# Block 1's attention, context squares and last key and query rotations re-divided among the engines of a two-block kernel

## The chip, the cores and the metric

One core of one Trainium2 chip runs the kernel. The metric is the device time of one execution in microseconds (us), the median of several runs. The engines are TensorE (PE in the rows, PEld for its weight loads), VectorE (DVE), ScalarE (ACT), GpSimd (POOL) and the queue of SyncE (SPq), which issues most DMAs.

## The reference

256 tokens of width 2048 go through two transformer blocks in fp32. The first block is the one whose attention the change touches:

```python
h = rms_norm(x, pre_mix_g[l])
z = h @ w_in[l]                       # q, k, v (8 heads of 128) and u (1024 wide)
a = chunked_attention(q, k, v, rel_bias[l])   # chunks of 64, scores * 128**-0.5 + bias
p = multiscale_pool(u, pool_w[l], pool_scale[l])  # trailing means over 2, 4, 8, 16 tokens minus the token, then a 256x256 map per group
m = jnp.concatenate([a, p], axis=-1) @ w_o[l]
x = x + rms_norm(m, post_mix_g[l])
h = rms_norm(x, pre_ffn_g[l])
up = causal_dwconv(h @ w_up[l], conv_w[l], conv_b[l])
y = (gelu(up[..., :D_FF]) * up[..., D_FF:]) @ w_down[l]
x = x + rms_norm(y, post_ffn_g[l])
```

The bias is added to the scaled scores and depends on query minus key position alone, clipped at 128 either way. The second block takes x and a context of 256 tokens: both are normalized and modulated (six vectors from `silu(c) @ w_ada`), keys and values of both come from w_in2, keys and queries are normalized per head and rotated (rope), 16 heads attend with a softmax (branch A) and 8 with a difference of two softmaxes (branch B), two gated branch products are added and go through w_out, and a gated feed-forward follows.

## The kernel before

Everything is kept with features on the partitions: an activation is 16 tiles of 128x256. Each weight matrix is read in units of 128x1024 (`raw`, 512 KB) into a ring of four. ScalarE rounds a unit to fp32r (`whi`, line 560), VectorE takes the rest (`wlo`, line 1027), and TensorE multiplies: high by high, high by low and low by high, 24 products a unit (lines 1622 to 1624, or 1608 to 1611 where a stage puts both halves in one PSUM bank). A `Stage` is one weight matrix or a part of it; its body is one turn of a loop over output groups. Each engine walks the same list of stages, and for unit j+4 it works while TensorE multiplies unit j. Work that is not a weight product is put between the units by hand. A DMA of a unit waits for the low half of the unit that had its slot. VectorE also makes the modulation vectors from `cond_rows`, one 128x512 fused product and sum at a time (line 1170, `condition`), against four vectors of silu; the last of them, `cond_silu_tail`, lies in the PSUM bank `CT`.

**Block 1's attention** stands between the stages w_in and w_o. TensorE, when the last group of w_in is evacuated, turns the values (line 1676, 16 transposes, copied out by ScalarE in line 737). VectorE scales the queries (line 1298, `q_scaled`). Then 16 steps follow, one per head h and block of 128 queries b; step i has 128 keys for b=0 and 256 for b=1. The score is two products into one PSUM bank, queries by keys (line 1686) and a product of a flipped identity with a Hankel matrix of the bias (line 1688). VectorE reduces to the negated maximum (line 1313), ScalarE takes exp with its sum (line 746), VectorE the reciprocal (1306) and the multiply (1308), TensorE transposes the result (1700) and issues the score of step i+2, ScalarE copies (754), TensorE multiplies by the values (1711), and a finished head is split into its high (758) and low half (1318). In VectorE's queue the multiply of step i-1 stands ahead of the reduction of step i:

```python
if 1 <= i <= N:
    n = i - 1
    dve.wait_ge(exped, n + 1)
    dve.reciprocal(...)
    dve.tensor_scalar(R[:, 48 + n % 2, 0:w], ...).then_inc(probs, 1)
if i < N:
    dve.wait_ge(scored, i + 1)
    dve.tensor_reduce(SM[:, i % 2:i % 2 + 1], PS[:, i % 2, 0, 0:w], AX.X, ALU.max, negate=True)
```

GpSimd makes the pooled means of the four groups meanwhile (lines 493 to 503). After the last step TensorE does 8 pool products (line 1720), one at a time with ScalarE's high half (761) and VectorE's low half (1271) of each; TensorE waits for all 16 operand tiles, and w_o starts.

**Context squares.** In stage up1c ScalarE squares the context (line 800). GpSimd adds the 16 tiles of squares up to one in 8 operations (line 519), and TensorE sums that over partitions in the last body of stage up1b.

**Rotations.** In stage q (48 units, steps 0 to 47) and in stage gates (steps from 48 on) keys and queries come in 12 chunks. A rotation of a chunk needs its halves swapped by DMAs and is three operations, chunk by cosine, swapped by sine, and their sum. VectorE rotates chunks 6, 0, 7, 1, 8, 9 (`rotate`, lines 1419 to 1423), GpSimd chunks 2, 3, 4, 5, 10, 11 (`rotate_late`, lines 541 to 546). Chunks 10 and 11, of 128x1024, are branch B's queries. Branch A's scores begin at step 55 (line 1831), its softmax on VectorE in lines 1470 to 1480, its transposes on TensorE in line 1816. Branch B's scores begin at step 87.

**First branch.** Stage branch_a is a loop of four bodies of two groups; VectorE evacuates each group with line 1079. TensorE's `body` waits at a body's first group for one evacuation more than elsewhere, since in the first body the group before belongs to the gates, and for the operand tiles:

```python
pe.wait_ge(evac_done, group(st, b, gb) + (2 if st is st_ba and fresh and gb == 0 else 1))
```

## Time and profile before

| | |
|---|---|
| median of 3 runs | 2875.73 us (2875.54 to 2875.75) |
| profiled execution, its own time | 2876.91 us |
| its span | 2875.1 us, granted clock 0.994 |
| PE busy | 2811.4 us (98%), 19046 products |
| DVE / ACT busy | 1997.1 us (69%) / 1274.9 us (44%) |
| POOL busy | 86.0 us (3%) |
| DMA | 612.77 MB, 213 GB/s |
| `wlo` on DVE, one | 1233 ns, x864 |
| `whi` on ACT, one | 1060 ns, x864 |

A view of the trace gives a start in us from the span's beginning, a length, an engine, the line of the kernel, the operation and its tiles; in square brackets stands how long the engine was idle before it, and which engine's event ended the wait. A row with x8 merges eight instructions.

### The profile page before, as it was taken

How to read it: one execution, taken by the hardware profiler on the slowest of the kernel's cores; microseconds unless marked ns; L12 is line 12 of the kernel's file. 1: busy time of each engine (PE TensorE's matmuls, PEld its weight loads, DVE VectorE, ACT ScalarE, POOL GpSimd, SP SyncE). 2: the span in 40 equal slices, each digit the busy share in tenths (PEclk: the TensorE clock that was granted, in tenths of full speed). 3: DMA queues.
4: the chain of work that ended last, by engine and by line, in shares of the span. 5: the costliest groups of instructions: out<-in, count | busy, mean ns of one | idle time of the engine just before them, and what ended most of it. 6: DMA issues, size and time to landing. Idle time of an engine off the chain costs nothing.

```text
span 2875.1 us, 52879 instructions
## 1 busy us (share of the span) xinstructions
PE 2811.4 (98%) x19046; PEld 2575.8 (90%) x19046; DVE 1997.1 (69%) x3060; ACT 1274.9 (44%) x1587; POOL 86.0 (3%) x74
## 2 busy tenths in 40 slices
PE   8998899999999999999999999999989999999999
PEld 8998899998899988888889898899988888888888
DVE  6776789867799987666678667866665555555554
ACT  5344455544454444211344455654444444344443
POOL 0011000100000000000003100000000000000000
PEclk9999999999999999999999999999999999999999
DMA  8874678667888885577777655666656666666665
GB/s 306 273 246 126 214 264 275 192 181 247 258 265 273 275 269 174 178 239 241 263 228 246 209 168 159 211 186 181 183 154 185 188 186 187 188 184 187 186 188 163
DMA packets 211744, 612.77 MB, mean 213 GB/s; under 512 B 23472, under 2 KB 31792, under 8 KB 210992
## 3 DMA queue, kind: packets, MB, share of 16 engines
q1 hardware_dynamic: 199296, 591.49, 65.9%
q10 hardware_dynamic: 11008, 14.60, 1.6%
q0 software_dynamic: 1328, 5.24, 0.5%
q8 instruction: 64, 1.05, 0.1%
q14 instruction: 48, 0.39, 0.0%
HBM read 600.75 MB, written 5.77 MB: 211 GB/s over the span
## 4 chain that ended last, share of the span: by engine, by line
PE 88%; DVE 6%; issue 3%; DMA 2%; ACT 1%; DVEq 0%; SPq 0%; ACTq 0%
PE acc L1624 24%; PE acc L1620 24%; PE acc L1622 12%; PE acc L1623 12%; DMA cond_rows<-w_ada 2%; PE acc L1608 2%; PE acc L1610 2%; PE acc L1611 2%; PE sums L1823 1%; PE acc L1618 1%; DVE cond_rows L1170 1%; PE acc L1831 1%; DVE wlo L1027 1%; PE turned L1816 1%; PE acc L1617 1%
## 5 line engine op out<-in xcount | busy, mean ns | idle before, releaser
L1027 DVE TENSOR_TENSOR wlo<-raw,whi 128x1024 fp32r<-128x1024 f32 x864 | 1064.2, 1233 | 713.9 <-ACT whi L560 711.5
L560 ACT ACTIVATE whi<-raw 128x1024 fp32r<-128x1024 f32 x864 | 914.6, 1060 | 1363.0 <-PE acc L1624 1132.4
L1624 PE MATMUL acc<-operand,wlo 128*128 128x256 f32 (+1 forms) x4816 | 1396.3, 290 | 0.0
L1622 PE MATMUL acc<-operand,whi 128*128 128x256 f32 (+1 forms) x3136 | 925.7, 295 | 29.2 <-DVE wlo L1027 14.0
L1624 PEld LDWEIGHTS acc<-operand,wlo 128*128 128x128 f32 x4816 | 921.8, 191 | 14.6
L1623 PE MATMUL acc<-operand,whi 128*128 128x256 f32 (+1 forms) x3136 | 923.9, 295 | 0.0
L1622 PEld LDWEIGHTS acc<-operand,whi 128*128 128x128 f32 x3136 | 603.4, 192 | 43.7 <-issue 25.4
L1623 PEld LDWEIGHTS acc<-operand,whi 128*128 128x128 f32 x3136 | 603.4, 192 | 12.7
L1620 PE MATMUL acc<-operand,whi 128*128 128x512 f32 x1680 | 599.9, 400 | 6.1 <-DVE operand L1385 5.7
L1620 PE MATMUL acc<-ffn_act,whi 128*128 128x512 f32 x1344 | 472.0, 395 | 0.0
L1620 PEld LDWEIGHTS acc<-operand,whi 128*128 128x128 f32 x1680 | 316.7, 189 | 81.7 <-issue 6.8
L1624 PE MATMUL acc<-ffn_act,wlo 128*128 128x256 f32 x1344 | 376.9, 280 | 0.0
L1620 PEld LDWEIGHTS acc<-ffn_act,whi 128*128 128x128 f32 x1344 | 252.0, 187 | 57.9
L1624 PEld LDWEIGHTS acc<-ffn_act,wlo 128*128 128x128 f32 x1344 | 254.0, 189 | 1.4
L1170 DVE CUSTOM_DVE_ANT_0 cond_rows<-cond_rows,cond_silu,cond_sums 128x512 f32<-128x512 f32 x252 | 191.5, 760 | 8.4 <-DMA cond_rows<-w_ada 6.4
L1608 PE MATMUL acc<-operand,whi 128*128 128x256 f32 x512 | 160.6, 314 | 0.0
L1611 PE MATMUL acc<-operand,wlo 128*128 128x256 f32 x512 | 145.0, 283 | 0.0
L1610 PE MATMUL acc<-operand,whi 128*128 128x256 f32 x512 | 144.9, 283 | 0.0
L1608 PEld LDWEIGHTS acc<-operand,whi 128*128 128x128 f32 x512 | 98.2, 192 | 20.3 <-issue 19.5
L1610 PEld LDWEIGHTS acc<-operand,whi 128*128 128x128 f32 x512 | 98.2, 192 | 8.2 <-issue 8.2
L1611 PEld LDWEIGHTS acc<-operand,wlo 128*128 128x128 f32 x512 | 98.1, 192 | 0.0
L1170 DVE CUSTOM_DVE_ANT_0 cond_rows<-cond_rows,cond_silu_tail,cond_sums 128x512 f32<-128x512 f32 x126 | 93.6, 743 | 6.3 <-DMA cond_rows<-w_ada 4.6
(220 smaller groups left out, 2005.2 us busy)
## 6 DMA issues: line engine op xcount, KB each, us to landing
cond_rows<-w_ada SPq DMA_DIRECT2D x512, 256.0 KB, 4.3
raw<-w_in SPq DMA_DIRECT2D x224, 512.0 KB, 3.6
raw<-w_up SPq DMA_DIRECT2D x176, 512.0 KB, 4.5
raw<-w_down SPq DMA_DIRECT2D x88, 512.0 KB, 3.7
raw<-w_fg SPq DMA_DIRECT2D x88, 512.0 KB, 3.8
raw<-w_fu SPq DMA_DIRECT2D x88, 512.0 KB, 3.5
raw<-w_fd SPq DMA_DIRECT2D x88, 512.0 KB, 3.5
raw<-w_o SPq DMA_DIRECT2D x32, 512.0 KB, 3.8
```

Source lines behind the costliest of these rows:

```text
L560: act.activation(whi[j % RING][:], raw[j % RING][:], ACT.Copy).then_inc(hi_done, 1)
L1027: dve.tensor_tensor(wlo[j % RING][:], raw[j % RING][:], whi[j % RING][:].bitcast(F32), ALU.subtract).then_inc(lo_done, 1)
L1170: dve.tensor_tensor_reduce(out=rows, in0=rows, in1=(staged_parts if st is st_up1c else silu_parts)[kr], scale=1.0, scalar=CA[:, h - 1:h] i ...
L1608: pe.matmul(half, h[:, x, f], mov[:, 0], start=first and m == 0, stop=False, skip_group_check=True)
L1610: pe.matmul(half, h[:, x, f], mov[:, 1], start=False, stop=False, skip_group_check=True)
L1611: ins = pe.matmul(half, l[:, x, f], mov[:, 0], start=False, stop=last, skip_group_check=True)
L1617: pe.matmul(out_, l[:, x, f], mov[:, 0], start=False, stop=False)
L1618: ins = pe.matmul(both, h[:, x, f], mov, start=False, stop=True)
L1620: pe.matmul(both, h[:, x, f], mov, start=first, stop=False)
L1622: pe.matmul(out_, h[:, x, f], mov[:, 0], start=first, stop=False)
L1623: pe.matmul(out_, h[:, x, f], mov[:, 1], start=False, stop=False)
L1624: ins = pe.matmul(out_, l[:, x, f], mov[:, 0], start=False, stop=last)
```

## The change

- The additions of the context squares leave GpSimd. VectorE does them as 8 operations in the first two bodies of up1b, after units 1, 2, 5 and 6.
- Chunks 10 and 11 are rotated by VectorE, one operation at each of the steps 48, 50, 52 and 58, 60, 62. Those who waited for GpSimd's sum wait for VectorE's.
- TensorE's first body of branch_a is written out, and only it has the stronger waits.
- In block 1's attention the value transposes go into the last body of w_in (after units 1, 3, 5, 6), which is written out on TensorE and ScalarE. The scale of the queries goes into the evacuation of w_in's first four groups; for that VectorE's first body is written out. The bias is read as one matrix of 128x256 per head and added by VectorE in the same instruction that takes the maximum; its result (`R[:, 64 + b]`) is what exp reads. The score is one product and waits for that instruction of step i-2, not for exp. In VectorE's queue the new instruction of step i stands ahead of the multiply of step i-1.
- The pool products go into steps 8 to 15, into the banks of `NB` and `CT`. What `CT` held is made anew by ScalarE behind the attention.

The diff's core, in the kernel's order of lines (indentation reduced):

```diff
def joined(st):
...
+TURNS_A = {6: 1, 0: 2, 7: 3, 1: 4, 8: 5, 9: 6, 10: 7, 11: 8}
+TURNS_B = {2: 1, 3: 2, 4: 3, 5: 4}
+TURN_AT = {48: (10, 0), 50: (10, 1), 52: (10, 2), 58: (11, 0), 60: (11, 1), 62: (11, 2)}
...
-    pool.wait_ge(sq_ready, SQ[5][0])
-    n, turn = KT // 2, 0
-    while n:
-        pool.wait_ge(poolstep, count)
-        for k in range(0, n, 2):
-            pool.wait_ge(hi_done, unit(st_up1b, turn // st_up1b.upb, turn % st_up1b.upb) + 1)
-            turn += 1
-            a, b = (XC32[:, x + k:x + min(k + 2, n), 1, 1, :] for x in (0, n))
-            step(pool.tensor_tensor(a, a, b, ALU.add))
-        n //= 2
-    pool.wait_ge(poolstep, count)
-    pool.sem_inc(acc_ready, 1)
...
-    for c in (2, 3, 4, 5, 10, 11):
+    for c in (2, 3, 4, 5):
...
+    def keep_values(j):
+        act.wait_ge(vt_turned, j + 1)
+        act.activation(R[:, 40 + 2 * j:42 + 2 * j, :], TP[:, j % 2, :].rearrange("p (a n) -> p a n", a=2),
+                       ACT.Copy).then_inc(vt_copied, 1)
+    with act.Fori(0, st_in.bodies - 1) as b:
+        body(st_in, b)
+    body(st_in, st_in.bodies - 1, then={at: lambda j=j: keep_values(j) for j, at in enumerate((2, 4, 6, 7))})
...
-            act.activation(R[:, 48 + i % 2, 0:w], PS[:, i % 2, 0, 0:w], ACT.Exp, bias=SM[:, i % 2:i % 2 + 1],
+            act.activation(R[:, 48 + i % 2, 0:w], R[:, 64 + i % 2, 0:w], ACT.Exp, scale=-1.0,
+                           bias=SM[:, i % 2:i % 2 + 1],
                            accum_out=SM[:, 2 + i % 2:3 + i % 2]).then_inc(exped, 1)
         if 1 <= i <= N:
...
-    for j in range(8):
-        act.wait_ge(summed, N + j + 1)
-        act.activation(XC[:, 8 + j, 0, 0, :], PS[:, j % 2, 1, 0:S], ACT.Copy,
-                       scale=V[:, VEC["pool_scale"] + j:VEC["pool_scale"] + j + 1]).then_inc(op_hi, 1)
+        if 10 <= i < 18:
+            j = i - 10
+            act.wait_ge(pool_summed, j + 1)
+            act.activation(XC[:, 8 + j, 0, 0, :], pool_sum(j), ACT.Copy,
+                           scale=V[:, VEC["pool_scale"] + j:VEC["pool_scale"] + j + 1]).then_inc(op_hi, 1)
+    act.wait_ge(opnd, 2 * KT)
+    act.activation(CT[:], staged_parts[3], ACT.Silu).then_inc(silu_done, 1)
     act.activation(SM[:, 36:37], SM[:, EPS_C:EPS_C + 1], ACT.Sqrt)
     run(st_o)
...
-            if k == "scale":
+            if k == "scale" and (st is st_inh or first):
+                dve.scalar_tensor_tensor(out=R[:, ds(tile, 2), :], in0=sums, scalar=HD ** -0.5,
+                                         in1=rep(RS[:], 2), op0=ALU.mult, op1=ALU.mult).then_inc(evac_done, 1)
...
-    run(st_in)
+    body(st_in, 0, first=True)
+    with dve.Fori(1, st_in.bodies) as b:
+        body(st_in, b)
...
-    dve.tensor_scalar(R[:, 0:8, :], R[:, 0:8, :], HD ** -0.5, None, ALU.mult).then_inc(q_scaled, 1)
-    clear(RS[:])
     N = 2 * H1
     for i in range(N + 4):
+        if i < N:
+            h, b = divmod(i, 2)
+            w = 128 * (b + 1)
+            dve.wait_ge(scored, i + 1)
+            if i >= 2:
+                dve.wait_ge(exped, i - 1)
+            dve.tensor_tensor_reduce(out=R[:, 64 + b, 0:w], in0=PS[:, b, 0, 0:w],
+                                     in1=bias(h)[:, P * (1 - b):P * (1 - b) + w], scale=-1.0, scalar=3e38,
+                                     op0=ALU.add, op1=ALU.min, accum_out=SM[:, b:b + 1]).then_inc(neg_max, 1)
...
             dve.tensor_scalar(R[:, 48 + n % 2, 0:w], R[:, 48 + n % 2, 0:w], SM[:, 4 + n % 2:5 + n % 2], None,
                               ALU.mult).then_inc(probs, 1)
-        if i < N:
-            w = 128 * (i % 2 + 1)
-            dve.wait_ge(scored, i + 1)
-            dve.tensor_reduce(SM[:, i % 2:i % 2 + 1], PS[:, i % 2, 0, 0:w], AX.X, ALU.max,
-                              negate=True).then_inc(neg_max, 1)
...
-    for j in range(8):
-        scaled_lo(8 + j, gain_col("pool_scale", j), KT + H1 + j + 1, PS[:, j % 2, 1, 0:S])
+        if 11 <= i < 19:
+            j = i - 11
+            scaled_lo(8 + j, gain_col("pool_scale", j), made(HI_ORDER, "pool", j), pool_sum(j))
+    clear(RS[:])
     clear(Zp[:, :, 0:2])
+    dve.wait_ge(silu_done, 5)
     run(st_o)
...
     body(st_up1c, 0, final=True)
-    run(st_up1b)
+    sums = [(n, k, min(k + 2, n)) for n in (8, 4, 2, 1) for k in range(0, n, 2)]
+    def add_squares(i):
+        n, k0, k1 = sums[i]
+        dve.wait_ge(sq_ready, SQ[5][0])
+        if n < 8:
+            dve.wait_ge(ctx_added, [x[0] for x in sums].index(n))
+        dst, src = (XC32[:, x + k0:x + k1, 1, 1, :] for x in (0, n))
+        dve.tensor_tensor(dst, dst, src, ALU.add).then_inc(acc_ready if n == 1 else ctx_added, 1)
+    for b in range(2):
+        body(st_up1b, b, then={at: lambda i=4 * b + x: add_squares(i) for x, at in enumerate((1, 2, 5, 6))})
+    with dve.Fori(2, st_up1b.bodies) as b:
+        body(st_up1b, b)
     dve.wait_ge(root_ready, 4)
     dve.reciprocal(CR, CR).then_inc(rstd_ready, 1)
     dve.wait_ge(rstd_ready, 4)
-    dve.wait_ge(silu_done, 9)
+    dve.wait_ge(silu_done, 10)
...
-    def rotate(c):
+    def rotate(c, parts=range(3)):
...
+        if 0 in parts:
+            if c < NK:
+                dve.wait_ge(k_swap[c % 2], swapped(c))
+            else:
+                dve.wait_ge(q_swap[c % 2], swapped(c))
+                dve.wait_ge(n_sq, job_of[c] + 1)
+                dve.wait_ge(n_table, 4)
+            dve.tensor_tensor(chunk, chunk, rep(cos, *dims), ALU.mult).then_inc(n_t1, 1)
+        if 1 in parts:
+            dve.tensor_tensor(sw, sw, rep(sin, *dims), ALU.mult).then_inc(n_t2, 1)
+        if 2 in parts:
+            dve.wait_ge(n_t1, n)
+            dve.wait_ge(n_t2, n)
+            dve.tensor_tensor(chunk, chunk, sw, ALU.add).then_inc(n_rope, 1)
...
-            if c in TURNS_A and c >= NK:
+            if c in TURNS_A and NK <= c < 10:
                 rotate(c)
+        if s in TURN_AT:
+            rotate(TURN_AT[s][0], TURN_AT[s][1:])
...
-    run(st_in)
-    pe.wait_ge(in_cst, 32)
...
-    for j in range(4):
+    def turn_values_1(j):
+        if j == 0:
+            pe.wait_ge(evac_done, groups_before(st_in) + 10)
         if j >= 2:
             pe.wait_ge(vt_copied, j - 1)
         for x in range(4):
             h, tb = 4 * (j % 2) + x, j // 2
             ins = pe.transpose(TP[:, j % 2, P * x:P * x + P], R[:, 16 + h, P * tb:P * tb + P], ident)
         ins.then_inc(vt_turned, 1)
-    pe.wait_ge(q_scaled, 1)
+    with pe.Fori(0, st_in.bodies - 1) as b:
+        body(st_in, b)
+    body(st_in, st_in.bodies - 1, then={at: lambda j=j: turn_values_1(j) for j, at in enumerate((1, 3, 5, 6))})
...
-            pe.wait_ge(exped, n - 1)
-        pe.matmul(PS[:, n % 2, 0, 0:w], R[:, h, P * b:P * b + P], R[:, 8 + h, 0:w], start=True, stop=False)
-        pe.matmul(PS[:, n % 2, 0, 0:w], flip, hankel(h)[:, P * (1 - b):P * (1 - b) + w], start=False,
+            pe.wait_ge(neg_max, n - 1)
+        else:
+            pe.wait_ge(evac_done, evacuated(st_in) - 1 + n)
+        pe.matmul(PS[:, n % 2, 0, 0:w], R[:, h, P * b:P * b + P], R[:, 8 + h, 0:w], start=True,
                   stop=True).then_inc(scored, 1)
...
-    for j in range(8):
-        g = j // 2
-        pe.wait_ge(pooled, g + 1)
-        pe.wait_ge(opnd, KT + H1 + j - 1)
-        for c in range(2):
-            ins = pe.matmul(PS[:, j % 2, 1, 0:S], R[:, 32 + 2 * g + c, P * (j % 2):P * (j % 2) + P],
-                            R[:, 24 + 2 * g + c, :], start=c == 0, stop=c == 1)
-        ins.then_inc(summed, 1)
+        if 8 <= i < 16:
+            j = i - 8
+            if j == 0:
+                pe.wait_ge(in_cst, 32)
+                pe.wait_ge(cond_used, COND_SLOTS + st_o.ib * COND_PARTS)
+            pe.wait_ge(pooled, j // 2 + 1)
+            if j >= 2:
+                pe.wait_ge(opnd, made(LO_ORDER, "pool", j - 2))
+            for c in range(2):
+                ins = pe.matmul(pool_sum(j), R[:, 32 + 2 * (j // 2) + c, P * (j % 2):P * (j % 2) + P],
+                                R[:, 24 + 2 * (j // 2) + c, :], start=c == 0, stop=c == 1)
+            ins.then_inc(pool_summed, 1)
...
-    run(st_ba)
+    body(st_ba, 0)
+    with pe.Fori(1, st_ba.bodies) as b:
+        body(st_ba, b, fresh=False)
```

## Rows read from the trace of the kernel before

**Rows 1.** three windows: stretch, length, busy us of PE, PEld, DVE, ACT, POOL; clock
```profile
560.00:600.00 40.00, 40.00 (x336) 40.00 (x335) 26.25 (x34) 19.71 (x24) 0.00 (x0) 1.00 0.64 188
...
203.06:230.78 27.72, 20.03 (x121) 17.01 (x122) 18.99 (x50) 14.75 (x49) 25.77 (x32) 0.94 0.17 55
211.30:214.30 3.00, 3.00 (x12) 2.64 (x11) 0.87 (x3) 1.22 (x6) 2.75 (x4) 0.50 0.02 5
```

**Rows 2.** TensorE's waits, whole span: us, times, longest
```profile
PE turned L1816 <- DVE operand_scratch L1480: 6.4, 1, 6.4
...
PE acc L1622 <- DVE tiles L1079: 3.1, 3, 1.0
```

**Rows 3.** timeline, block 1's attention begins (start, us, engine, line, operation)
```profile
203.00 0.86 PEld L1676 LDWEIGHTS turned<-ident_ones,tiles 128*128 128x128 f32 x8 [1.14 <-issue]
...
205.44 1.23 DVE L1298 TENSOR_SCALAR tiles<-tiles 128x2048 f32<-128x2048 f32 x1
...
207.54 0.29 DVE L1313 TENSOR_REDUCE small<-acc 128x1 f32<-128x128 f32 x1 [0.60 <-PE acc L1688]
```

**Rows 4.** timeline of its last head, a pool product, w_o's start
```profile
230.97 0.42 DVE L1313 TENSOR_REDUCE small<-acc 128x1 f32<-128x256 f32 x1
...
232.02 0.16 DVE L1306 RECIPROCAL small<-small 128x1 f32<-128x1 f32 x1 [0.63 <-ACT tiles L746]
...
232.22 0.35 DVE L1308 TENSOR_SCALAR tiles<-tiles,small 128x256 f32<-128x256 f32 x1
...
232.90 0.60 PE L1686 MATMUL acc<-tiles 128*128 128x256 f32 x2
...
233.97 0.43 DVE L1313 TENSOR_REDUCE small<-acc 128x1 f32<-128x256 f32 x1 [0.18 <-PE acc L1688]
...
238.28 2.12 PE L1720 MATMUL acc<-tiles 128*128 128x256 f32 x8 [0.16 <-DVE operand L1318]
...
247.68 0.36 PE L1622 MATMUL acc<-operand,whi 128*128 128x256 f32 x1 [1.47 <-DVE operand L1271]
```

**Rows 5.** VectorE by line and shape, 190 to 250 (busy us, mean ns)
```profile
L1308 DVE TENSOR_SCALAR tiles<-tiles,small 128x256 f32<-128x256 f32 x8 | 5.4, 676 | 0.3
...
L1313 DVE TENSOR_REDUCE small<-acc 128x1 f32<-128x256 f32 x8 | 3.4, 423 | 1.9 <-PE acc L1688 1.5
...
L1308 DVE TENSOR_SCALAR tiles<-tiles,small 128x128 f32<-128x128 f32 x8 | 3.3, 412 | 0.3
...
L1313 DVE TENSOR_REDUCE small<-acc 128x1 f32<-128x128 f32 x8 | 2.2, 280 | 0.6 <-PE acc L1688 0.6
...
L1170 DVE CUSTOM_DVE_ANT_0 cond_rows<-cond_rows,cond_silu,cond_sums 128x512 f32<-128x512 f32 x3 | 2.2, 746 | 0.0
```

**Rows 6.** the timeline of the stop at 534 us
```profile
524.87 11.80 POOL L519 TENSOR_TENSOR operand_scratch<-operand_scratch 128x512 f32<-128x512 f32 x8 [149.35 <-ACT operand_scratch L800]
...
528.58 5.83 DVE L1120 SCALAR_TENSOR_TENSOR conv_out<-conv_in,vectors,conv_out 128x256 f32<-128x256 f32 x4
...
538.87 0.58 PE L1622 MATMUL acc<-operand,whi 128*128 128x256 f32 x1 [4.67 <-DVE wlo L1027]
...
542.24 0.30 PE L1622 MATMUL acc<-operand,whi 128*128 128x256 f32 x1
```

**Rows 7.** the timeline of the stop at 1600 us
```profile
1594.38 2.20 DVE L1170 CUSTOM_DVE_ANT_0 cond_rows<-cond_rows,cond_silu,cond_sums 128x512 f32<-128x512 f32 x1 [0.61 <-DMA cond_rows<-w_ada]
...
1596.51 3.39 DVE L1027 TENSOR_TENSOR wlo<-raw,whi 128x1024 fp32r<-128x1024 f32 x1
...
1600.83 1.30 DVE L1473 TENSOR_TENSOR small<-small,operand_scratch 128x1 f32<-128x1 f32 x1
...
1606.68 1.11 PE L1816 MATMUL turned<-ident_ones,operand_scratch 128*128 128x128 f32 x4 [6.40 <-DVE operand_scratch L1480]
...
1610.58 0.32 PE L1608 MATMUL acc<-operand,whi 128*128 128x256 f32 x1
```

**Rows 8.** VectorE by line and shape, 560 to 1125, two SBUF sources
```profile
L1149 DVE TENSOR_TENSOR conv_out<-conv_out,gate_act 128x512 f32<-128x512 f32 x14 | 9.7, 692 | 0.5
```

More of the change, by code:

```diff
@@ L222, in build @@
         scr = lambda kt: XC32[:, kt, :, 1, :]
-        flip = XC32[:, 13, 0, 1, 0:128]
         halves = XC32[:, 13, 0, 1, 128:256]
         CR = R[:, 55, :]
-        hankel = lambda h: XC32[:, h // 2, h % 2, 1, :]
+        bias = lambda h: XC32[:, h // 2, h % 2, 1, :]
         poolfix = XC32[:, 13, 1, 1, :]
@@ L268, in build @@
         mod_t, mod_v, mod_hi, gains = sem("mod_scaled"), sem("mod_value"), sem("mod_hi"), sem("gains")
-        q_scaled, vt_turned, vt_copied, masked, pooled, poolstep = (
-            sem(n) for n in ("q_scaled", "vt_turned", "vt_copied", "masked", "pooled", "poolstep"))
+        pool_summed = sem("pool_summed")
+        vt_turned, vt_copied, masked, pooled, poolstep = (
+            sem(n) for n in ("vt_turned", "vt_copied", "masked", "pooled", "poolstep"))
         scored, neg_max, exped, inverse, probs, turned, pt_copied, summed = (
@@ L318, in grouped @@
             return unit(st, b, st.last[gb]) + 1 + RING
+        HI_ORDER = [x for i in range(2 * H1 + 3) for x in (([("head", (i - 3) // 2)] if i >= 3 and i % 2 else [])
+                                                            + ([("pool", i - 10)] if 10 <= i < 18 else []))]
+        LO_ORDER = [x for i in range(2 * H1 + 4) for x in (([("head", (i - 4) // 2)] if i >= 4 and i % 2 == 0 else [])
+                                                            + ([("pool", i - 11)] if 11 <= i < 19 else []))]
+        made = lambda order, what, i: KT + order.index((what, i)) + 1
         staged = R[:, Yt:Yt + 8, :].rearrange("p a n -> p (a n)")
@@ L472, in _ @@
             pool.wait_ge(in_att, 64)
-            pool.memset(XC32[64:128, 0:4, :, 1, 192:256], -1e30).then_inc(masked, 1)
+            pool.memset(XC32[0:64, 0:4, :, 1, 192:256], -1e30).then_inc(masked, 1)
             pool.wait_ge(masked, 1)
@@ L1040, in steps_from, with evac @@
                 return did, settled
-            def evac(st, b, gb):
+            def evac(st, b, gb, first=False):
                 g = group(st, b, gb)
@@ L1211, in context_operand, with body @@
                                       XC[:, ds(4 * b, 4), 0, 1, :].bitcast(F32), ALU.subtract).then_inc(opnd, 4)
-            def body(st, b, final=False, norm=None, then={}):
+            def body(st, b, final=False, norm=None, then={}, first=False):
                 for j in range(RING, RING + st.upb):
@@ L1222, in body @@
                     if gb is not None and not gate:
-                        evac(st, b, gb)
+                        evac(st, b, gb, first)
                     if j < st.upb or not final:
@@ L1626, in multiply, with body @@
                     ins.then_inc(used, 1)
-            def body(st, b, fresh=True, insert=None):
+            def body(st, b, fresh=True, insert=None, then={}):
                 for j, (gb, u) in enumerate(st.entries):
@@ L1636, in body @@
                         sum_squares(insert)
+                    if j in then:
+                        then[j]()
             def run(st):
@@ L1664, in _ @@
             body(st_inh, 0, insert=0)
-            run(st_in)
-            pe.wait_ge(in_cst, 32)
-            pe.wait_ge(evac_done, evacuated(st_in))
-            pe.wait_ge(masked, 1)
-            for j in range(4):
+            def turn_values_1(j):
+                if j == 0:
+                    pe.wait_ge(evac_done, groups_before(st_in) + 10)
                 if j >= 2:
@@ L1708, in _ @@
                     if b == 0 and h >= 2:
-                        pe.wait_ge(opnd, KT + h - 1)
+                        pe.wait_ge(opnd, made(LO_ORDER, "head", h - 2))
                     for t in range(b + 1):
@@ L1987 @@
     reach = a["rel_bias"].shape[2] // 2
-    order = np.clip(S - 1 - np.arange(S + P - 1), -reach, reach) + reach
+    order = np.clip(P + np.arange(P)[:, None] - np.arange(S)[None, :], -reach, reach) + reach
     arrays = {
         "xT": feature_major(a["x"][0]), "ctxT": feature_major(a["ctx_2"][0]), "vec": np.ascontiguousarray(vec),
-        "cst": constants(), "rel": np.ascontiguousarray(a["rel_bias"][0][:, order]), "w_in": by_block(a["w_in"][0]),
+        "cst": constants(), "rel": np.ascontiguousarray(a["rel_bias"][0][:, order].transpose(1, 0, 2)), "w_in": by_block(a["w_in"][0]),
         "pool_w": np.ascontiguousarray(a["pool_w"][0].reshape(8, P, 256).transpose(1, 0, 2)),
```

41 lines of the change are left out of this document (12 added, 29 removed).

## The prediction

> **What bounds the kernel now.** I read the windows first: in a stretch without a stop (560 to 600) TensorE is busy all 40 us and VectorE 26 [rows 1]. A change to VectorE, ScalarE or GpSimd can therefore only give back time in which TensorE stands, or runs at half clock. So the second view is who TensorE waited for in the whole span of 2875.1 us; of its rows two matter here, 6.4 us in one piece before the first transpose of the second block's attention and 3.1 us in three pieces for a VectorE evacuation in the first branch [rows 2]. The third view is the timeline around each part of the change.
>
> Block 1's attention is a serial chain between four engines, 207.54 to 233.97 us by its first and last reduction, then 8 pool products that end in the first product of w_o at 247.68 [rows 3, 4]. In its last head, where GpSimd is silent, one turn takes 3.00 us (230.97 to 233.97): reduction 0.42, exp with its sum and the reciprocal 0.83 (to the multiply at 232.22), multiply 0.35, transposes up to the score 0.33, score 0.60, bias product 0.43 [rows 4, 5]. Earlier turns are longer since the multiply L1308 averages 676 and 412 ns where alone it takes 350, and by estimate 280 in the narrow form (as L1313 does) [rows 4, 5]; GpSimd works 25.77 of the 27.72 us from 203.06 to 230.78 [rows 1].
>
> Elsewhere GpSimd's additions of context squares (11.80 us from 524.87) stretch VectorE's low halves until TensorE stops from 534.20 to 538.87 and then runs at 1.2 GHz to 542.24 [rows 6]. GpSimd's rotation of chunk 11 stretches three VectorE instructions from 1594.38 on, and this ends in the stop from 1600.28 to 1606.68 and a half clock to 1610.6 [rows 7].
>
> **Part 1, context squares.** Removed: 8 GpSimd additions. Added: 8 VectorE additions of 128x512, 0.69 us each by the like form L1149 [rows 8], 5.5 us in all, four in each of two bodies of some 23 us (8 units of 24 products 0.12 apart: 336 in 40 us [rows 1]). Without GpSimd the low half for which TensorE stopped comes after short taps: the four that took 5.83 from 528.58 take no more than four times 0.69, then three instructions of a product and its split at 0.7 and the low half at 1.2. That is 534.6 by this bound, where TensorE wants it at 534.04; the taps are half as wide as L1149, so I expect 533.5 and no stop. The next ones are wanted every 2.9 us and cost 1.2 plus an addition of 0.7. So the additions lie beside TensorE and cost nothing; if that cover were gone they would cost at most 5.5 us less what was idle. The stop gives 534.04 to 538.87, 4.8 us; the slow stretch ran 16 products in 3.37 us instead of 1.92, 1.45 more. **Gain 6.3** (5 to 6.3).
>
> **Part 2, last rotations.** Chunk 10's three passes go to steps 48, 50, 52 and chunk 11's to 58, 60, 62 on VectorE, 0.69 plus 512 columns at 1.1 ns, 1.2 us each [rows 5, 8]; chunks 2 to 5 stay on GpSimd. The waits that move with them are for the swap of each chunk; the later one had landed when GpSimd stretched VectorE at 1594.38 [rows 7], before step 58. Behind each pass on VectorE stand a reduction of the attention and a weight's low half; TensorE has three units of weights in hand. Chunk 10's passes replace longer delays that GpSimd caused there. What is late next is VectorE's first softmax step: the fused instruction took 2.20 instead of 0.75, the low half 3.39 instead of 1.2, the negated scale L1473 1.30 instead of 0.16, the length of so small an operation (L1306) [rows 4, 5, 7]. Taken away, this brings the end of the stop from 1606.68 to 1601.9, where TensorE is free at 1600.3. I leave 2.0 of the 6.4 us standing; a stop so short should leave the clock at 2.4 GHz, as the three of a microsecond in the branch are not followed by slow products. The slow stretch 1606.68 to 1610.6 at half rate cost 2.0. **Gain 6.4**, between 0 (the rotations delay the same softmax as much) and 8.4.
>
> **Part 3, branch body peeled.** In the loop every body waits for the evacuation just before it; peeled, only the first does. Removed are the 3 stops of 1.03 us, 3.1 us [rows 2]. The others wait on an evacuation two groups back, long done. **Gain 3.1** (up to 0.4 more, since a restart costs a product's fill each time). The added instructions of the bodies written out are costed at nothing: TensorE's queue shows no stop at the seams that are already there.
>
> **Part 4, attention.** Step by step:
> - Moved ahead: 16 transposes of values into the last body of w_in, where TensorE has no idle time. 8 take 0.86 us [rows 3], so everything behind shifts by 1.7. ScalarE's four copies there lie in its idle time.
> - Removed: the query scaling L1298, 1.23 us, and its 0.87 wait behind [rows 3]; the scale rides in evacuations of the same length. The first reduction can start where L1298 did: 205.44 plus 1.7 is 207.1, against 207.54.
> - Removed: the bias product, 0.43 in a wide step. Added: an addition fused with the reduction. A fused product over 128x512 takes 746 ns [rows 5]; less 256 columns at 1.1 ns (L1313 takes 423 and 280 ns for 256 and 128) that is 0.46, and with 0.02 for its two sources 0.48, against 0.42.
> - Reordered: VectorE now reduces step i before it takes the reciprocal and multiply of step i-1. Its turn becomes multiply, transposes, score, reduction, reciprocal, and that per step, not per head. Wide: 0.35+0.33+0.60+0.48+0.20 (L1306 starts 0.20 before the multiply [rows 4]) = 1.96. Narrow, with half the columns, 1.44. Sum 3.40 a head, where 3.00 less 0.43 plus 0.06 would be 2.63 with the old order. Seven heads and the first 0.4 make 24.2.
> - Kept: the multiply's delay by GpSimd, (676-350) x 8 plus (412-280) x 8 = 3.7, and 0.6 for a piece of half clock as at 211.3 to 214.3 [rows 1]. Last reduction: 207.1+24.2+3.7+0.6 = 235.6.
> - The pool products now run inside steps 8 to 15. TensorE's own work in a head is under 1.6 (0.33 and 0.60 in the wide step, half in the narrow one, and values not longer than the score) plus two products of at most 1.1 (238.28 to 247.68 holds eight with their halves, 1.2 each [rows 4]), so it hardly exceeds the turn and adds nothing. The fourth pooled group is ready at 230.8+1.7 = 232.5, and its product stands behind the transposes of step 14, about 234: hidden by 1.5.
> - Tail: 4.3 as before (233.97 to 238.28), 0.9 for the last pool product ahead of the last values, 0.9 for its two halves behind the head's: 6.1. Then 0.4 to the first product as now: w_o starts at 242.1 instead of 247.68. The Silu of the rows that the second pool buffer overwrote and its table load run while four units of weights are ready. **Gain 5.6**.
>
> Bounds of part 4: the fused reduction of a PSUM and an SBUF operand is in no row. If the multiply's delays vanish, 9.3; if the fused one takes 0.1 more and the delays grow by a third, 2.6; below that are the rivals. I take 0.48 since it is the same kind of instruction.
>
> What GpSimd blocks is told by rows: L1308 and L1027 (sources in SBUF alone) are stretched, L1313 (source in PSUM) keeps 423 ns [rows 5, 7]. By that the new reduction, with one operand in each, is not delayed. The Trainium skill (GPSIMD Engine Reference, Key points) says that GpSimd shares its SBUF interfaces with VectorE and contends with instructions that have two SBUF inputs or run in a two-port mode; by that rule too it is free, and the trace agrees as far as those rows go.
>
> **Sum.** 6.3+6.4+3.1+5.6 = 21.4 us. The profiled execution took 2876.91 us, 1.8 outside its span and 1.2 over the median; the terms are differences, so I take them from the median: 2875.73 - 21.4 = 2854.3.
>
> **Rivals.**
> - A, attention gains nothing: without the bias products TensorE is sparser in the first eight steps, and the clock falls to 1.2 GHz there, as it did after 202 to 211. Transposes and score (0.93) at half rate add 0.9 to a wide and 0.5 to a narrow step, 5.6 in four heads: 2859.9. For it: the dip at 211.3 [rows 1]. Against: the later steps were as thin and kept 2.4 GHz. The Trainium skill (TensorE: Matmul & The Clock Gate, What's actually happening) makes the clock a matter of how busy TensorE has recently been; that speaks for A and its price is the same 5.6. 0.14.
> - B, VectorE's rotations keep the first softmax as late as now: 21.4 less 6.4, 2860.7. For it: VectorE waits there for weight rows too. Against: GpSimd's stretching alone is 4.7 us of the three rows. 0.13; A and B together 0.02, 2866.3.
> - C, slower: each fused reduction is held by GpSimd as other fused ones are (one took 2.20 beside the rotation, 1.5 more [rows 7]). Sixteen on the chain at x each cost 16x; the gain is gone at x = 1.34 and the kernel is over 0.2% slower from 1.70; at the 2.2 by which the low half was stretched it is 35, 2889.5 in all. Against: L1313's 423 ns. 0.05, of which 0.02 slower and 0.02 unchanged.
> - The parts do what they say: every wait moved is on the same event or a later one, so a change without effect is left inside B.
>
> **Numbers.** Forecast 0.66. 0.2%, 5.8 us, is what a measurement here can tell from no change. Faster 0.66+0.14+0.13+0.02+0.01 = 0.96, same 0.02, slower 0.02. The range goes from all terms near their best (27.5 in all) to beyond A and B singly with a short fused delay (13): 2848 to 2863.
>
> **What would show it.** No GpSimd work at 525 to 537 and from 1563 on; TensorE without a stop near 534 and without the three at branch starts; the stop before L1816 at 1 to 2 us; first reduction 0.4 earlier relative to the span's start, 3.4 us a head in quiet stretches, w_o's first product near 242. Wrong if the turns are 3.0 or 4 us, if the fused reduction is far from 0.48 us beside GpSimd, if the granted clock stays 0.5 before step 8, or if a new stop stands in gates steps 10 to 14.

## The result and the profile after

The changed kernel takes 2856.53 us (median of 4 runs, 2854.43 to 2859.76); the kernel before, run beside it, 2875.74 (2875.54 to 2875.88). The ratio is 0.9931, interval 0.9919 to 0.9944: 19.2 us less, where 2854.3 in a range of 2848 to 2863 was forecast. The profiled execution took 2856.53 us, with a span of 2854.7 against 2875.1, 20.4 less. Where these came from can be read at landmarks that both kernels have, by how much earlier each comes:

| landmark on TensorE | before | after | earlier |
|---|---|---|---|
| first product of w_o | 247.68 | 245.46 | 2.2 |
| first context product (kvh) | 1125.1 | 1117.3 | 7.9 |
| first score of branch A | 1592.6 | 1583.9 | 8.7 |
| first score of branch B | 1760.1 | 1744.0 | 16.1 |
| end of the span | 2875.1 | 2854.7 | 20.4 |

So the attention gave 2.2 us, the stretch with the context squares 5.7, the one up to branch A's first score 0.8, the one with the last rotations 7.4, and the rest, with the branch's bodies, 4.3. The 5.7 hides a loss. Just ahead of the context products TensorE stands 2.13 us in both kernels, and only in the changed one it then runs at half clock (clock 0.50 in the window 1116 to 1118), as the four sums there show, first before, then after:

```profile
1124.35 1.13 PE L1650 MATMUL sums<-conv_out,ident_ones 128*128 128x256 f32 x4 [2.13 <-ACT conv_out L582]
```

```profile
1115.75 2.07 PE L1681 MATMUL sums<-conv_out,ident_ones 128*128 128x256 f32 x4 [2.13 <-ACT conv_out L573]
```

Up to these sums the changed kernel is 8.6 us earlier, so the squares' stretch gave 6.4, of which 0.7 went to this half clock. TensorE's waits in the whole span of the changed kernel (for whom; us, times, longest):

```profile
PE acc L1651 <- DVE wlo L1026: 10.3, 2, 9.0
PE acc L1651 <- DVE operand L1273: 9.2, 2, 7.5
PE turned L1731 <- DVE tiles L1320: 8.2, 7, 3.8
...
PE turned L1851 <- DVE operand_scratch L1509: 0.8, 2, 0.4
```

The 6.4 us before the second block's first transpose are two waits of 0.4 and the three of 1.0 at the branch's bodies are gone; both stood in [rows 2]. What is left in the attention is one wait of 3.8 us and six short ones. The windows of the changed kernel (stretch, length, busy us of PE, PEld, DVE, ACT, POOL, then the granted clock) say what this costs:

```profile
205.00:240.00 35.00, 26.77 (x114) 21.53 (x115) 19.95 (x77) 18.31 (x60) 25.28 (x32) 0.66 0.12 43
207.80:231.30 23.50, 17.50 (x61) 14.00 (x62) 11.18 (x46) 9.76 (x35) 21.79 (x29) 0.50 0.08 32
```

For 23.5 us TensorE has 0.50 of its clock, 1.2 GHz; before, the stretch 203.06 to 230.78 had 0.94 [rows 1]. This is rival A. The timeline shows it in the operations (start, length, engine, line): first the start of the attention, then a head at half clock, then the last head at full clock:

```profile
204.87 0.70 PE L1719 MATMUL acc<-tiles 128*128 128x256 f32 x2 [0.69 <-DVE tiles L1072]
...
207.53 0.29 DVE L1311 CUSTOM_DVE_ANT_0 tiles<-acc,operand_scratch 128x128 f32<-128x128 f32 x1 [0.17 <-issue]
...
209.36 0.45 PE L1731 MATMUL turned<-ident_ones,tiles 128*128 128x128 f32 x1 [3.79 <-DVE tiles L1320]
...
211.58 1.06 PE L1719 MATMUL acc<-tiles 128*128 128x256 f32 x2
...
212.67 0.42 DVE L1311 CUSTOM_DVE_ANT_0 tiles<-acc,operand_scratch 128x256 f32<-128x256 f32 x1 [1.64 <-PE acc L1719]
...
216.93 0.42 DVE L1311 CUSTOM_DVE_ANT_0 tiles<-acc,operand_scratch 128x256 f32<-128x256 f32 x1 [0.70 <-PE acc L1719]
...
219.25 1.14 DVE L1320 TENSOR_SCALAR tiles<-tiles,small 128x256 f32<-128x256 f32 x1
...
235.60 0.42 DVE L1311 CUSTOM_DVE_ANT_0 tiles<-acc,operand_scratch 128x256 f32<-128x256 f32 x1 [0.25 <-PE acc L1719]
...
238.41 0.60 PE L1719 MATMUL acc<-tiles 128*128 128x256 f32 x2
...
239.05 0.42 DVE L1311 CUSTOM_DVE_ANT_0 tiles<-acc,operand_scratch 128x256 f32<-128x256 f32 x1 [0.25 <-PE acc L1719]
...
245.46 0.36 PE L1651 MATMUL acc<-operand,whi 128*128 128x256 f32 x1 [1.75 <-DVE operand L1273]
```

A head takes 4.26 us at half clock (212.67 to 216.93) and 3.45 at full clock (235.60 to 239.05). The same wide score takes 1.06 us and 0.60. The last reduction comes at 239.05, where 235.6 was forecast; behind it the 6.4 us to w_o are as forecast.

A second reading bears on rival C. The fused reduction keeps its length beside GpSimd, while the multiply, which reads and writes SBUF, does not (VectorE by line and shape, 205 to 236; busy us, mean ns):

```profile
L1311 DVE CUSTOM_DVE_ANT_0 tiles<-acc,operand_scratch 128x256 f32<-128x256 f32 x7 | 3.0, 424 | 6.3 <-PE acc L1719 6.3
L1320 DVE TENSOR_SCALAR tiles<-tiles,small 128x256 f32<-128x256 f32 x6 | 2.9, 485 | 0.2
L1320 DVE TENSOR_SCALAR tiles<-tiles,small 128x128 f32<-128x128 f32 x6 | 2.9, 476 | 0.2
```

Absolute times in a span differ by up to 1.7 us between profiled executions before the attention begins (first reduction at 206.72 in one, 208.42 in another, of kernels that are alike up to there). So below, the **attention's length** is taken from the first reduction to the first product of w_o. It is 40.1 us before (207.54 to 247.68 [rows 3, 4]) and 37.9 in the changed kernel; the forecast's terms make 35.0 (207.1 to 242.1).

### The profile page after: what moved, and what is told of

Same layout as the page of the kernel before. It is cut to its first block, busy times and chain, and to the rows that moved or that the text cites. A ratio compares the mean times of both kernels' runs of the same rounds, so it can differ in the third digit from the quotient of the medians.

```text
span 2854.7 us, 52735 instructions
## 1 busy us (share of the span) xinstructions
PE 2806.8 (98%) x19014; PEld 2573.3 (90%) x19014; DVE 1986.5 (70%) x3089; ACT 1279.4 (45%) x1589; POOL 54.7 (2%) x60
## 4 chain that ended last, share of the span: by engine, by line
PE 96%; DVE 2%; ACT 1%; issue 0%; DMA 0%; DVEq 0%; ACTq 0%
PE acc L1653 27%; PE acc L1649 25%; PE acc L1651 14%; PE acc L1652 14%; PE acc L1637 2%; PE acc L1640 2%; PE acc L1639 2%; PE sums L1858 2%; PE acc L1647 1%; PE acc L1866 1%; PE turned L1851 1%; PE acc L1646 1%; PE sums L1807 1%; PE acc L1902 1%; PE sums L1691 1%
```

## The experiments

Two questions stood: whether the clock is what took the attention's gain, and whether the other three terms are worth what the landmarks say. The first four kernels went on one chip, the next four on one, the last four on one. The kernel before had medians of 2877.19 (2874.44 to 2879.20), 2877.85 (2875.03 to 2878.47) and 2876.15 us (2874.80 to 2878.49) there, so a difference of a microsecond between medians is not read.

### The attention alone

The squares, the rotations and the branch's loop are put back as in the kernel before; the attention stays changed.

> Only the attention's part of the change (part 4); squares, rotations and branch body as before. By the forecast's sum it gains 5.6 us: 2870.1. By the clock theory (TensorE at 1.2 GHz for most of the attention, seen in the changed kernel) it gains what w_o's first product gained there, 2.2 us: 2873.5, with the granted clock near 0.5 from about 208 to 231 again. If the three other parts had a share in the shift of w_o's first product, that product would come at another time than 245.5.

2874.82 us (2871.99 to 2878.20, 10 runs) beside 2877.19, ratio 0.9994 (0.9985 to 1.0004). The medians are 2.4 us apart, but the interval holds no change and leaves out 5.6 us. In its profile the attention's length is 35.8 us, and the clock is 0.80 over 205 to 240: it falls near the same place (209.4 instead of 207.8), but comes back for a while in between. w_o's first product is 3.9 us earlier than before and the end of the span 2.0 (2873.1); the 1.9 between were given back in small pieces, among them a longer half clock behind the stop of the context squares and one at 1131 to 1134 that the kernel before has not. So the attention as the change writes it is worth about 2 us in these runs, not 5.6; its own end, w_o's first product, gained up to 3.9.

### Products that nobody reads

```diff
+            def keep_busy(n):
+                for _ in range(n):
+                    pe.matmul(NB[:, S:S + 256], ones, IO[:, 0:256], start=True, stop=True)
             score(0)
             score(1)
+            keep_busy(6)
...
                 if i + 2 < N:
                     score(i + 2)
+                if i < 8:
+                    keep_busy(1)
```

> The changed kernel with products that nobody reads: six of 128x256 in TensorE's stop after the second score and one in each of the first eight steps, to keep TensorE busy. Clock theory: the granted clock stays above 0.9 from 208 to 234, the last reduction comes near 235.6 instead of 239.05 and w_o's first product near 242, 3.4 us less, about 2853. Rival (the length of the turns is GpSimd's delays and VectorE's queue, the clock is not what costs): clock back at 1.0 and the last reduction still near 239, time 2856 to 2857. If the fillers themselves stand in the way, later still.

2850.46 us (2850.32 to 2851.16), ratio 0.9911 (0.9894 to 0.9927), some 6 us below the changed kernel, with 14 products added. The two were never run beside each other, but each was run in two places, and the fastest of the changed kernel's eight runs (2853.87) is slower than the slowest of this one's eight (2851.16). The windows of this kernel, to be laid beside those of the changed one:

```profile
205.00:240.00 35.00, 28.67 (x163) 23.53 (x164) 23.67 (x86) 21.77 (x68) 25.14 (x32) 1.00 0.13 43
207.80:231.30 23.50, 19.06 (x111) 15.31 (x110) 15.66 (x62) 13.60 (x48) 21.79 (x29) 1.00 0.09 32
```

and its timeline (the six fillers, each of two passes; the first reduction; a step's filler behind its score; w_o):

```profile
205.44 2.75 PE L1724 MATMUL sums<-ident_ones 128*128 128x256 f32 x12
...
207.56 0.29 DVE L1311 CUSTOM_DVE_ANT_0 tiles<-acc,operand_scratch 128x128 f32<-128x128 f32 x1 [0.17 <-issue]
...
209.39 0.30 PE L1736 MATMUL turned<-ident_ones,tiles 128*128 128x128 f32 x1 [1.20 <-DVE tiles L1320]
...
211.04 0.60 PE L1719 MATMUL acc<-tiles 128*128 128x256 f32 x2
211.48 0.59 PE L1724 MATMUL sums<-ident_ones 128*128 128x256 f32 x2
...
239.92 0.36 PE L1651 MATMUL acc<-operand,whi 128*128 128x256 f32 x1 [1.75 <-DVE operand L1273]
```

GpSimd's busy time in the window is the same 21.79 us, the instructions of VectorE are the same, the clock is 1.00 instead of 0.50, and the attention's length is 32.4 us instead of 37.9. The rival, that GpSimd's delays set the length, falls. The gain is larger than expected: w_o's first product comes at 239.9, not 242. This run and its repetition below also spread by 0.8 and 0.6 us, where the changed kernel spreads by 5 to 6.

### VectorE's order of before

```diff
             for i in range(N + 4):
-                if i < N:
-                    ... fused reduction of step i
                 if 1 <= i <= N:
                     ... reciprocal and multiply of step i-1
+                if i < N:
+                    ... fused reduction of step i
```

> The changed kernel with VectorE's order of before: reciprocal and multiply of step i-1 ahead of the fused reduction of step i. Theory 1: the new order put the transposes and the score on the chain (3.45 us a head at 2.4 GHz and 4.3 at 1.2); with the old order the chain is reduction, exp, reciprocal, multiply, next reduction, 2.9 us a head by 0.42+0.83+0.35 and 0.29+0.7+0.28, whatever TensorE's clock: last reduction near 232 to 233, w_o's first product near 239, time about 2850. Theory 2 (what sets the turn is TensorE at half clock in either order): 4 us a head stays in the half-clock stretch, last reduction within 1 us of 239.05, 2856. The forecast's own estimate of the old order was 2.63 a head.

2849.55 us (2849.09 to 2851.85), ratio 0.9909 (0.9893 to 0.9926). The attention's length is 30.7 us. Two heads in VectorE's timeline, at full clock with GpSimd at work:

```profile
220.03 0.17 DVE L1309 RECIPROCAL small<-small 128x1 f32<-128x1 f32 x1 [0.67 <-ACT tiles L741]
220.23 0.35 DVE L1311 TENSOR_SCALAR tiles<-tiles,small 128x256 f32<-128x256 f32 x1
220.50 0.28 DVE L1319 CUSTOM_DVE_ANT_0 tiles<-acc,operand_scratch 128x128 f32<-128x128 f32 x1
...
223.04 0.39 DVE L1311 TENSOR_SCALAR tiles<-tiles,small 128x256 f32<-128x256 f32 x1
223.35 0.28 DVE L1319 CUSTOM_DVE_ANT_0 tiles<-acc,operand_scratch 128x128 f32<-128x128 f32 x1
```

Its first product of w_o:

```profile
238.12 0.35 PE L1651 MATMUL acc<-operand,whi 128*128 128x256 f32 x1 [1.74 <-DVE operand L1273]
```

VectorE now waits for ScalarE's exp (0.67), not for TensorE's score: the reduction follows the multiply without a gap. A head takes 2.85 us (220.50 to 223.35) against the 2.9 expected, and against 3.45 in the change's order. With TensorE off the chain the steps also come closer together, and the clock is at 0.50 only from 208 to about 214, 0.86 over 207.80 to 231.30. Theory 1 stands, with one reservation: at half clock a head still took 3.6 us (210.40 to 213.96). VectorE waited 0.36 of it for a score, so TensorE is not wholly off the chain there; a slower multiply (0.62 us) is another 0.27.

This run says something more on the cause. It has no bias product either, and from 214.3 on it keeps 2.4 GHz, as the kernel before does. So the missing product alone does not explain 23.5 us at half clock; the longer turn of the change's order has a part in it, as far as one profile can say (`e11` below is a second). How large a part is not shown, since the new order was not run with the bias product.

### Both

> Both edits of the two runs before. Theory 1 (old order takes TensorE off the chain): no gain of the fillers over the old order alone, within 0.5 us at w_o's first product. Theory 2 (half clock sets the turn): the fillers bring w_o's first product several us forward against the old order alone, to about 240.

2847.99 us (2847.38 to 2850.12), ratio 0.9903 (0.9887 to 0.9920): the lowest median of all, 1.6 us below the order alone, while the ranges overlap. The attention's length is 29.4 us, 1.3 less than with the order alone, clock 1.00 throughout. w_o's first product comes 0.9 us earlier than with the order alone (237.24 against 238.12), where theory 1 allowed 0.5 and theory 2 wanted several. The fillers give 5.5 us of length in the change's order and 1.3 in the old one: what the clock costs depends on whether TensorE is on the chain.

### Squares, rotations and branch loop put back, one at a time

The base is the kernel with fillers, whose runs agree best. `e5` gives the additions back to GpSimd and leaves them out of VectorE's bodies, `e6` gives chunks 10 and 11 back to `rotate_late`, `e7` has `run(st_ba)` instead of the body written out.

> The kernel with fillers and the change's own order (2850.5 us, all its runs within 0.9), with the context squares' additions back on GpSimd (part 1 undone). Forecast's term: the stop at up1b and its half clock return, 6.3 us more (5 to 6.3), 2856.8; by the shift of the latent's first context products between the two traces, 5.7. Rival (the stop has another cause, such as the weights' arrival): 2850.5.

> The same base with the rotations of chunks 10 and 11 back on GpSimd (part 2 undone). Forecast's term 6.4 more (0 to 8.4), 2856.9; by the shift of the first score of branch B between the two traces 7.3, 2857.8. Rival B of the prediction (VectorE's rotations hold the softmax as much): no change, 2850.5.

> The same base with the first branch's body back in the loop (part 3 undone). Forecast's term 3.1 more (to 3.5), 2853.6 to 2854.0, three stops of 1.03 us back at body starts. Rival (peeling moves the wait to another place, or the stop is made up for later by the weights): under 1 us.

> The base of the three runs before, on their chip: 2850.5 as before, within 1 us, w_o's first product at 239.9 and the granted clock 1.0 through the attention. If its runs spread by over 2 us here, the clock elsewhere makes the spread and the three differences are worth no more than that.

| kernel | median (range), us | span, us | over the base: median, span |
|---|---|---|---|
| base again | 2851.03 (2850.56 to 2851.11) | 2848.8 | |
| squares on GpSimd | 2857.25 (2856.24 to 2857.91) | 2855.5 | 6.2, 6.7 |
| rotations on GpSimd | 2857.31 (2856.19 to 2859.07) | 2855.6 | 6.3, 6.8 |
| branch body in the loop | 2856.09 (2854.50 to 2858.37) | 2852.7 | 5.1, 3.9 |

Each stop is back at its place in TensorE's waits. With the rotations on GpSimd:

```profile
PE turned L1862 <- DVE operand_scratch L1513: 4.8, 1, 4.8
```

and with the branch body in the loop:

```profile
PE acc L1651 <- DVE tiles L1081: 3.1, 3, 1.0
```

With the squares on GpSimd a stop of 4.2 us stands from 526.25 to 530.47 while one GpSimd group (11.81 us) runs from 516.92. The rivals that the stops have other causes, and that VectorE's rotations hold the softmax as much, fall. In the branch the stops are 3.1 us; from the first product of stage branch_a to the sums behind w_out the kernel takes 234.8 instead of 231.1 us, so each of three restarts costs about 0.2 more. The median says 5.1, but the runs of that kernel spread by 3.9 us. A span holds what differs elsewhere too: w_o's first product comes 0.1 us earlier, 0.7 later and 0.7 earlier than in the base, and half clocks behind other stops are longer in one profile than in another. So for the branch's loop the 3.7 of its own stretch is the best reading.

### The changed kernel again, and the stop filled alone

> The changed kernel itself, on the chip of the three runs beside it. Clock theory: 2856 to 2857 median with a spread of several us (2854.4 to 2859.8 so far), since the half-clock stretch of the attention is there in every run and varies; with fillers the spread was 0.9.

> The changed kernel with the six unread products in TensorE's stop of 3.8 us, and none in the steps. If the stop is what loses the clock, the granted clock stays 1.0 through the attention and w_o's first product comes at 240, time 2850.5 as with all fillers. If the thin steps lose it (rival A as the prediction put it), the clock falls to 0.5 within the first eight steps and w_o's first product lies between 241 and 245, time 2852 to 2856.

The changed kernel: 2856.98 us (2853.87 to 2860.05), ratio 0.9932 (0.9915 to 0.9948), attention 37.4 us, clock 0.80 over 205 to 240 where the first profile had 0.66. With the stop filled and no product in the steps: 2855.14 us (2851.67 to 2856.34), ratio 0.9923 (0.9906 to 0.9939), attention 36.9 us. TensorE's stop is down from 3.8 to 1.2 us, and still the clock falls as soon as the steps run, at 0.69 in the window 209 to 211 and 0.50 in the two behind it, and again from 223 to 230. The long stop is not needed to lose the clock; the thin steps lose it, as rival A had it. The 36.9 us are no gain to read: the three profiles with the stop unfilled have 35.8 (`e1`), 37.4 and 37.9.

### The value transposes out of w_in's body again

```diff
-            body(st_in, st_in.bodies - 1, then={at: lambda j=j: turn_values_1(j) for j, at in enumerate((1, 3, 5, 6))})
+            body(st_in, st_in.bodies - 1)
+            turn_values_1(0)
+            turn_values_1(1)
...
             score(1)
+            turn_values_1(2)
+            turn_values_1(3)
```

ScalarE's four copies stand together ahead of its first exp, and VectorE has the old order.

> The changed kernel with VectorE's old order, and the 16 transposes of values taken out of w_in's last body again: two groups before the first score, two after the second, ScalarE's copies before its first exp. By the forecast's term the transposes in w_in's body cost 1.7 us; behind it they lie in TensorE's stop: first reduction near 205.8, less up to 0.6 for ScalarE (four copies and the table load come before the exp), w_o's first product 1.2 to 1.7 earlier than with the order alone (238.1): 236.7, 2848. Rival (the first reduction waits for VectorE's other work and for ScalarE, and the shift is lost): 238.1, 2849.5.

> The same with four unread products in the stop and one in each of the first eight steps. If all effects add: w_o's first product at 237.2 less 1.2 to 1.7, 235.8, and 2846.5, the fastest of all; if the transposes alone fill the stop enough to keep the clock, no better than the kernel beside it without fillers.

2850.61 us (2849.70 to 2852.84) and 2850.46 (2849.35 to 2850.95), ratios 0.9912 (0.9896 to 0.9929) and 0.9909 (0.9893 to 0.9926): nothing gained. w_o's first product comes at 238.35 and 238.91, where 236.7 and 235.8 were hoped for and the old order alone has 238.12. The first reduction did come earlier, at 205.94 and 205.83 where the eleven profiles with the transposes in w_in's body have 206.72 to 208.42, but not the second. Rows from ScalarE's and VectorE's timeline without fillers:

```profile
204.75 1.08 ACT L716 ACTIVATE tiles<-turned 128x512 f32<-128x512 f32 x2 [0.26 <-PE turned L1706]
205.85 1.28 ACT L743 ACT_TABLE_LOAD   x1
207.15 0.40 ACT L743 ACTIVATE tiles<-tiles,small 128x128 f32<-128x128 f32 x1
```

```profile
205.94 0.29 DVE L1321 CUSTOM_DVE_ANT_0 tiles<-acc,operand_scratch 128x128 f32<-128x128 f32 x1 [0.17 <-issue]
...
207.88 1.09 DVE L1313 TENSOR_SCALAR tiles<-tiles,small 128x128 f32<-128x128 f32 x1
208.89 0.41 DVE L1321 CUSTOM_DVE_ANT_0 tiles<-acc,operand_scratch 128x256 f32<-128x256 f32 x1
```

The exp waits for the copies and a table load of 1.28 us, and the multiply behind it takes 1.09 us beside GpSimd. The second reduction is at 208.89, where it was at 208.65 with the same order and the transposes in w_in's body; with four fillers ahead of the last transposes it is at 210.12. The rival stands. In the change the copies and the load are out of the way by the time of the first reduction, which here makes up for the 1.7 us that the transposes cost in w_in. With fillers the clock still fell to 0.55 and 0.59 in the windows from 211 to 215 here; with the transposes in w_in it did not.

## Why the prediction was right or wrong

**The total** was right in sign and size, 19.2 us against 21.4. The likeliest case was not the one that happened: parts 1 to 3 went as forecast, and part 4 went as rival A had it, whose 2859.9 was 3.4 too high, mostly because the attention still gained 2.2 us. That the total came so near is in part luck: the attention gave 3.4 less than its 5.6, and the rest of the kernel 1.2 more than its 15.8 by the medians (2.4 by the two profiles). A sign that the prediction named for being wrong, the clock at 0.5 before step 8, did appear, and in that stretch a turn took 4.26 us and more.

**Part 1, squares: right.** Forecast 6.3, measured 6.2 by putting them back, 5.7 by the landmarks and 6.4 without the half clock ahead of the context products. VectorE's additions take 0.69 us each, as estimated (the last, of one tile, 0.42), and no stop stands there.

**Part 2, rotations: right, a little small.** Forecast 6.4, of a range 0 to 8.4; measured 6.3 by putting them back, about 7.4 by the landmarks. The step "I leave 2.0 of the 6.4 us standing" was mis-sized: two waits of 0.4 are left, where the sign to look for was a stop of 1 to 2 us. A pass takes 1.22 us as estimated.

**Part 3, body peeled: right.** Forecast 3.1, up to 0.4 more; measured 3.1 of stops and 0.6 of restarts, 3.7.

**Part 4, attention: the step that failed is "0.6 for a piece of half clock as at 211.3 to 214.3".** I took the clock of the kernel before over into a kernel whose TensorE has 0.43 us less to do in each wide step, and gave the clock's fall a rival's chance of 0.14. It fell in both profiles of the changed kernel and in that of the attention alone. In the first one it stayed at 1.2 GHz from 207.8 to 231.3, and this is the term that missed: with the clock held by fillers the attention takes 32.4 us against 35.0 forecast and 37.9 unheld. The argument against rival A, that the later steps of before were as thin and kept 2.4 GHz, did not carry: those steps held the bias product too, and ran in a turn of 3.00 us, while the new order's turn is 3.45. Of the two differences the turn has a part: without the product too, the old order kept its clock from about 214.5 on in both kernels that have it and no fillers (`e3` and `e11`), while the new order lost it again or had not got it back by then in all four profiles without products in the steps. Which of the two weighs more stays open. The price set on A was near: 5.6 against the 5.5 by which the two lengths differ (5.0 by the second profile). It is made up otherwise, and not of 1.4 a head over four: 0.81 us a head over five heads is 4.1; the fifth has some 0.9 on top, since the first pool product, at half clock, takes 1.91 us (229.38) and stands ahead of its transposes; about 0.6 is left, as the delayed multiplies fall otherwise in the two profiles. Their sum is not larger in the changed kernel (2.0 us over the plain lengths, 2.4 with fillers). What kept the attention from losing its whole gain is that the forecast's other terms were 2.0 too dear: 35.0 less the 0.6 for half clock is 34.4, against 32.4 measured where the clock held.

The page TensorE: Matmul & The Clock Gate (What's actually happening) of the Trainium skill, cited for rival A, makes the clock follow how busy TensorE has been. The runs agree: over 207.8 to 231.3 the clock is 1.00 with the added products, 0.50 and 0.75 in the two profiles without them, with nothing else changed.

**The other terms of part 4, read where the clock held** (the base, second run):
- First reduction 207.41, forecast 207.1.
- A head 3.44 us (229.94 to 233.38), forecast 3.40; so the price of 0.48 for the fused reduction held in sum. Its row says 424 ns, with 83 ns for reading the accumulator beside it.
- The multiply's delays were forecast at 3.7. Of eight wide and eight narrow multiplies the means are 368 and 569 ns, and by the same reckoning (over 350 and 280) that is 2.5, of which the chain from first to last reduction (25.97, less 24.2) shows 1.8.
- Tail 6.4 us, forecast 6.5.
- Rival C is false: the fused reduction takes 424 ns beside GpSimd and 424 at the quiet end.

**Not costed as a choice.** The prediction did see that the new order lengthens the turn, "3.40 a head, where ... 2.63 with the old order". It took this as given and did not ask what else hangs on it: putting transposes and score on the chain is also what makes the half clock dear (5.5 us against 1.3), and the longer turn helps to make it long. Its 2.63 is too low; the old order gives 2.85, since the chain is then reduction, exp, reciprocal and multiply, and not the turn of before less the bias product.

**Left open.** Why the half-clock stretch of the changed kernel is 23.5 us long in one execution and in two pieces in another isn't known; nor why the kernel before has no half clock around its first context products, when every other profile but that of `e7` has one. How much of the 5 to 6 us spread comes from it isn't known, since where the clock falls shows only in the profiled executions. The mean granted clock over a whole execution is on record for all, and it goes with the time: of the first four runs of the changed kernel the fastest (2854.43) has 0.996 and the slowest (2859.76) 0.992, while all eight with fillers have 0.996 or 0.997. The kernel before spread by 3 to 5 us on the three later chips as well.

## What to carry to other kernels

Work taken from TensorE in a chain of small steps must be priced twice: what it took, and what the clock takes if TensorE becomes too sparse. Here the attention would have been 7.7 us shorter with the clock held, the second price ate all but 2.2 of it, and 14 unread products gave it back. When such a chain crosses engines, write out for each order of the queue which engines stand between one step and the next: of two orders with the same work, the one that keeps TensorE off the chain was 3.0 us shorter even at full clock (32.4 against 29.4), and lost least to half clock. An engine whose data-dependent stop is filled only at its longest place is not yet busy: with the 3.8 us stop alone filled the clock still fell, and the attention was no shorter than its other profiles are by chance.

## What the runs showed of the hardware

- A fused VectorE addition and minimum over 128x256, one operand in PSUM and one in SBUF, takes 424 ns, as long as the plain reduction of before (423 ns [rows 5]): the second operand adds nothing, and GpSimd does not stretch it. The 83 ns for reading its accumulator start together with the next instruction.
- The granted clock of the changed kernel went back to 1.00 at about 231.3, where pool products had just joined the steps. Products that serve nothing held it at 1.00. Whether fewer than one in each of the first eight steps would hold it wasn't tried.
- A score of 128x256 (two passes) takes 0.60 us at 2.4 GHz and 1.06 at 1.2 GHz. A head's turn grew from 3.45 to 4.26 us, by 0.81: only part of TensorE's work lies on the chain at either rate.
